# Three passes of rounded parts in the second layer's input projection, with two modulation chunks moved into the first layer's output projection

## The reference

```python
def first_block(x, c, ctx, c_ctx, w_ada, b_ada, g_norm, w_in, ...):
    for l in range(DEPTH):
        mod_lat = silu_c @ w_ada[l] + b_ada[l]
        mod_ctx = silu_cc @ w_ada[l] + b_ada[l]
        x, ctx = _layer(x, ctx, mod_lat, mod_ctx, tabs, g_norm[l], w_in[l], ...)
    return _rms_norm(x, g_final)
```

## Time and profile before

| | |
|---|---|
| runs | 1577.1 us median of 3 (1576.3 to 1580.47) |
| profiled execution, its own time | 1567.37 us |
| its span | 1565.6 us |
| granted TensorE clock, mean | 0.974 of full |
| busy share PE, DVE, ACT, POOL | 95%, 65%, 44%, 12% |
| second layer's input projection | 394.3 to 520.0 us |

### The profile page before, as it was taken

One profiled execution on the slowest core, in us unless ns is written; L12 is line 12 of the kernel. 1 busy time (PEld: TensorE's weight loads), 2 busy tenths in 40 slices (PEclk: granted clock), 3 DMA queues, 4 the chain that ended last, 5 costly groups with the idle time before them and its releaser, 6 DMA issues.

```text
span 1565.6 us, 19696 instructions
## 1 busy us (share of the span) xinstructions
PE 1481.6 (95%) x7621; PEld 1092.2 (70%) x7621; DVE 1010.9 (65%) x1587; ACT 695.9 (44%) x1125; POOL 192.0 (12%) x208
## 2 busy tenths in 40 slices
PE   5999997999999899999999999999999998899999
PEld 2777782554655455788778877878887876768886
DVE  2419747752475854677677768587786556477776
ACT  3311228322211631656146623466666657356654
POOL 1558721000000100200210010000000005000000
PEclk8999999999999989999999999899999999999999
DMA  9585611202484431766686654198884530098882
GB/s 339 193 259 199 223 62 55 82 1 98 145 293 160 165 121 55 234 215 219 189 238 233 224 172 105 55 324 297 311 302 139 188 108 1 1 307 305 292 305 108
DMA packets 186474, 286.55 MB, mean 183 GB/s; under 512 B 13739, under 2 KB 95115, under 8 KB 186380
## 3 DMA queue, kind: packets, MB, share of 16 engines
q1 hardware_dynamic: 172080, 273.56, 50.7%
q0 software_dynamic: 13200, 8.84, 3.0%
q10 hardware_dynamic: 1100, 2.89, 0.5%
HBM read 283.77 MB, written 1.49 MB: 182 GB/s over the span
## 4 chain that ended last, share of the span: by engine, by line
PE 80%; DVE 10%; ACT 5%; DMA 2%; SPq 1%; issue 1%; POOL 0%; DVEq 0%; ACTq 0%; POOLq 0%
PE ps L1309 40%; PE ps L2853 9%; PE ps L2744 3%; PE ps L2871 3%; PE ps L2873 2%; PE ps L2872 2%; DVE acc L2197 2%; DMA ring<-in_w_ada 2%; ACT ps L2045 2%; SPq L421 1%; PE ps L2777 1%; PE ps L2756 1%; PE ps L2765 1%; PE ps L2942 1%; PE ps L2982 1%
## 5 line engine op out<-in xcount | busy, mean ns | idle before, releaser
L1309 PE MATMUL ps<-WB,YP 128*128 128x512 f32 x1196 | 289.5, 396 | 2.7 <-DVE WB L2152 2.7
L1309 PEld LDWEIGHTS ps<-WB,YP 128*128 128x128 f32 x1196 | 228.0, 192 | 51.0 <-issue 2.2
L2152 DVE TENSOR_TENSOR WP<-ring,WP 128x2048 fp32r<-128x2048 f32 (+1 forms) x102 | 219.2, 2164 | 49.0 <-ACT WP L797 48.9
L1309 PE MATMUL ps<-WP,XP 128*128 128x512 f32 x960 | 233.1, 396 | 6.2 <-DVE WP L2152 6.2
L1309 PEld LDWEIGHTS ps<-WP,XP 128*128 128x128 f32 x960 | 178.8, 189 | 44.9 <-DVE XP L2152 4.9
L797 ACT ACTIVATE WP<-ring 128x2048 fp32r<-128x2048 f32 x94 | 179.5, 1914 | 38.2 <-PE ps L1309 38.2
L2152 DVE TENSOR_TENSOR WB<-ring,WB 128x512 fp32r<-128x512 f32 x192 | 128.0, 690 | 85.0 <-ACT WB L651 83.2
L2853 PE MATMUL ps<-ring,XT 128*128 128x512 f32 (+3 forms) x448 | 159.7, 511 | 2.6 <-ACT XT L1988 2.6
L651 ACT ACTIVATE WB<-ring 128x512 fp32r<-128x512 f32 x192 | 114.1, 628 | 53.9 <-PE ps L1309 53.9
L2853 PEld LDWEIGHTS ps<-ring,XT 128*128 128x128 f32 x448 | 81.7, 190 | 71.7 <-issue 63.6
L2197 DVE SCALAR_TENSOR_TENSOR acc<-ring,silu_c,acc 128x512 f32<-128x512 f32 x168 | 126.9, 756 | 4.4
(11 more groups left out here) (406 smaller groups left out, 2190.1 us busy)
## 6 DMA issues: line engine op xcount, KB each, us to landing
ring<-in_w_ada SPq DMA_DIRECT2D x72, 1024.0 KB, 7.4
ring<-in_a_w_in SPq DMA_DIRECT2D x36, 1024.0 KB, 5.0
ring<-in_w_gate SPq DMA_DIRECT2D x64, 512.0 KB, 4.2
ring<-in_w_up SPq DMA_DIRECT2D x64, 512.0 KB, 5.2
ring<-in_w_down SPq DMA_DIRECT2D x32, 1024.0 KB, 6.1
ring<-in_w_in SPq DMA_DIRECT2D x24, 1024.0 KB, 9.5
ring<-in_b_w_in SPq DMA_DIRECT2D x12, 1024.0 KB, 5.0
ring<-in_w_out SPq DMA_DIRECT2D x8, 1024.0 KB, 5.1
```

Source lines behind the costliest of these rows:

```text
L1309: ins = mm(dst, x(a), w(b), start=(start and n == 0), stop=(stop_ and n == 2))
L2152: return v.tensor_tensor(out_, a, b, op)
```

## The change

Chunks 2 to 6 of the second layer's projection (SPLIT = 2) are made in three passes of rounded parts, one weight block after the other for all tiles (`project_split_late`). ACT rounds the blocks (`high`) into 14 buffers (WH, the new WX, and XL, which lies on XT), DVE subtracts (`low`) into the ring slot itself; ACT also rounds the input into XH and DVE writes its low part (XL1) into unused columns of P. The blocks for chunk k + 1 are written into ACT's and DVE's queues ahead of chunk k's evictions and post-processing; those for chunk 2 behind the modulation of chunk 1. Modulations 3 and 4 move into the first layer's output projection, whose outputs now run through all tiles for the first 512 columns and then for the second; 5 to 9 stand behind chunks 0 to 4.

```diff
-               {0: (('ada2', 0, 3),), 1: (('ada2', 0, 4),), 2: (('ada2', 0, 5),), 3: (('ada2', 0, 6),), 4: (('ada2', 0, 7),), 5: (('ada2', 0, 8),), 6: (('ada2', 0, 9),)})
+               {n: (('ada2', 0, 5 + n),) for n in range(5)})
+MODS_OUT = (3, 4)
+SPLIT = 2
+HIGHS = 14
+def output_order(tiles):
+    return [(t, n) for n in range(2) for t in tiles] if len(tiles) == T else [(t, n) for t in tiles for n in range(2)]
...
     for n in range(2):
         chunk("wout", 0, n * 512, n * 512 + 512)
+    for c in MODS_OUT:
+        chunk("ada2", 0, c * 512, c * 512 + 512)
...
+                    if CHUNKS.index(it[2:4]) >= SPLIT:
+                        released.append(("w1_used", 7 * (CHUNKS.index(it[2:4]) - SPLIT) + 4))
...
+        W1H = [WH[:, n] for n in range(4)] + [WX[:, 0:512], WX[:, 512:1024]] + [XL[:, k] for k in range(KB)]
+        XL1 = [PH[:, at:at + 512] for at in (n + col for n in (0, D_IN) for col in (0, 512, BZ, CO))]
...
+                def high(r):
+                    it, w, hi, _ = win1_block(r)
+                    if r % 4 == 0:
+                        item_ready(act, it)
+                    if r == 6:
+                        act.wait_ge(*chunk_projected(SPLIT - 1))
+                        act.wait_ge(S("xt_lo"), 2 * KB)
+                    if r >= HIGHS:
+                        act.wait_ge(*win1_block_used(r - HIGHS))
+                    s_.activation(hi, w, ACT.Copy).then_inc(S("w1_hi"), 1)
+                for k in range(KB) if l == 1 else ():
+                    act.wait_ge(S("xt_act" if k % 2 == 0 else "xt_dve"), 4 + k // 2 + 1)
+                    s_.activation(XH[:, k], XT[:, k], ACT.Copy).then_inc(S("xt_hi"), 1)
                 for k, (lo, hi) in enumerate(CHUNKS):
+                    if l == 1 and SPLIT <= k < 6:
+                        for n in range(8):
+                            high(8 * (k + 1 - SPLIT) + n)
...
+                ops = (ada_ops("ada2", 0, ch) for ch in MODS_OUT)
+                for i, (t, n) in enumerate(output_order(tiles)):
+                    if len(tiles) == T:
+                        if i in (0, 5):
+                            chunk_ops = next(ops)
+                        for _ in range(0 if i in (4, 7) else 2 if i < 4 else 4):
+                            next(chunk_ops, None)
...
+                def low(r):
+                    _, w, hi, lo = win1_block(r)
+                    dve.wait_ge(S("w1_hi"), r + 1)
+                    tt(lo, w, hi.bitcast(F32), ALU.subtract).then_inc(S("w1_lo"), 1)
...
                 for k, (lo, hi) in enumerate(CHUNKS):
+                    if l == 1 and SPLIT <= k < 6:
+                        for n in range(8):
+                            low(8 * (k + 1 - SPLIT) + n)
                     for kind, layer, ch in MODS_BEHIND[l].get(k, ()) if l == 1 else ():
                         ada(kind, layer, ch)
+                    if l == 1 and k == 0:
+                        for n in range(KB):
+                            dve.wait_ge(S("xt_hi"), KB + n + 1)
+                            tt(XL1[n], XT[:, n], XH[:, n].bitcast(F32), ALU.subtract).then_inc(S("xt_lo"), 1)
+                    if l == 1 and k == SPLIT - 1:
+                        for n in range(6):
+                            low(n)
...
+            def project_split_late(n, behind):
+                lo_, hi_ = CHUNKS[n]
+                tiles = [(t, (lo_, hi_) if t >= 2 else CTX_LAST[n]) for t in range(T) if t >= 2 or CTX_LAST[n]]
+                us = [c.up("proj") - 1 for _ in tiles]
+                for k in range(KB):
+                    r = 8 * (n - SPLIT) + k
+                    _, _, hi, lo = win1_block(r)
+                    if n == SPLIT:
+                        pe.wait_ge(S("xt_lo"), KB + k + 1)
+                    pe.wait_ge(S("w1_lo"), r + 1)
+                    for (t, (a, e)), u in zip(tiles, us):
+                        if k == 0:
+                            pe.wait_ge(S("evict"), u - 3)
+                        b, cols, part = bank(u % 4, 0, e - a), slice(128 * t, 128 * t + 128), slice(a - lo_, e - lo_)
+                        mm(b, XH[:, k, cols], hi[:, part], start=(k == 0), stop=False)
+                        mm(b, XH[:, k, cols], lo[:, part], start=False, stop=False)
+                        ins = mm(b, XL1[k][:, cols], hi[:, part], start=False, stop=(k == KB - 1))
...
+                    if n == SIDE_CHUNK[1] and k in (1, 3, 5):
                         behind[k // 2]()
...
+                    pe.wait_ge(S("outp_used"), c.at("outp"))
                     norm_by_tile(range(T), before_last=5, before_chunks=3)
...
-                    if l == 1 and k > 0:
-                        ada(1)
-                    if l == 1 and k == 6:
+                    if l == 1 and k - 1 in MODS_BEHIND[1]:
                         ada(1)
```

More of the change, by code:

```diff
@@ L2094, in block1 @@
                             evict(P[:, t, rng[0]:rng[1]], lambda b, r=rng: b[:, 0:r[1] - r[0]])
+                        if l == 1 and k == SPLIT - 1 and t >= 2:
+                            for n in range(6) if t == 2 else range(6, 8):
+                                high(n)
                     if k < 6:
@@ L2494, in out_proj @@
                 dve.wait_ge(S("gate_rows_sb"), c.up("gate_rows_sb", len(set(side(t) for t in tiles))))
[L2495 to L2505, removed]
+                ops = (ada_ops("ada2", 0, ch) for ch in MODS_OUT)
[5 more added lines that the diff above has]
+                            next(chunk_ops, None)
+                        if i in (3, 6):
+                            a = c.up("ada") - 1
+                            pending.append(("ada2", 0, MODS_OUT[i // 4], a, bank(6 + a % 2, 0, 8)))
+                        if i in (5, 7):
+                            ada_cols()
+                    u = c.up("outp") - 1
+                    dve.wait_ge(S("outp"), u + 1)
+                    x = X[:, t, n * 512:n * 512 + 512]
+                    to("outp_used", tt(Ef[:, 0:512], bank((u + 2) % 4), GR[:, side(t), n * 512:n * 512 + 512], ALU.mult))
+                    ins = tt(x, x, Ef[:, 0:512], ALU.add)
+                    if n == 0:
+                        link(ins)
+                    else:
+                        to("x_tile", ins)
+                        (behind or (lambda t: invert_rstd([t])))(t)
             def twice_inverted(t):
@@ L2561, in block1 @@
                     dve.wait_ge(S("evict"), c.up("evict", units))
+                    if l == 1 and k == SPLIT - 1:
+                        low(6)
+                        low(7)
                     if before[1]:
@@ L2987, in out_proj @@
                 pe.wait_ge(S("evict"), c.at("proj"))
[L2988 to L2991, removed]
-                        if u - outp0[0] >= 4:
-                            pe.wait_ge(S("outp_used"), u - 3)
-                        b = bank((u + 2) % 4)
-                        if last_blocks and u == outp0[0]:
-                            project(b, t, its, 0, 512, 512, lhs=lhs, blocks=range(6))
-                            last_blocks()
-                            pe.wait_ge(S("evict"), c.at("proj"))
-                            ins = project(b, t, its, 0, 512, 512, lhs=lhs, blocks=range(6, 8))
-                        else:
-                            ins = project(b, t, its, 0, 512, 512, lhs=lhs)
-                        ins.then_inc(S("outp"), 1)
+                for i, (t, n) in enumerate(output_order(tiles)):
+                    its = [index[(kind, l, n * 512, n * 512 + 512, h)] for h in range(2)]
+                    u = c.up("outp") - 1
+                    if u - outp0[0] >= 4:
+                        pe.wait_ge(S("outp_used"), u - 3)
+                    b = bank((u + 2) % 4)
+                    if last_blocks and u == outp0[0]:
+                        project(b, t, its, 0, 512, 512, lhs=lhs, blocks=range(6))
+                        last_blocks()
+                        pe.wait_ge(S("evict"), c.at("proj"))
+                        ins = project(b, t, its, 0, 512, 512, lhs=lhs, blocks=range(6, 8))
+                    else:
+                        ins = project(b, t, its, 0, 512, 512, lhs=lhs)
+                    ins.then_inc(S("outp"), 1)
+                    if len(tiles) == T and i in (4, 6):
+                        ada(1)
                 outp0[0] = c.at("outp")
@@ L3111, in block1 @@
                         project_split(k, behind)
-                    for t in range(T) if l == 1 else ():
+                    elif k >= SPLIT:
+                        project_split_late(k, behind)
+                    for t in range(T) if l == 1 and k < SPLIT else ():
                         r = (lo, hi) if (l == 0 or t >= 2) else CTX_LAST[k]
```

23 lines of the change are left out of this document (18 added, 5 removed).

## The result

The changed kernel took 1585.4 us (median of 4 runs, 1582.9 to 1586.6) against 1576.7 for the kernel before: ratio 1.0048, 95% interval 1.0028 to 1.0068. It is slower, by 8.7 us where 12.3 were forecast, and measured again beside other runs by 9.6 us (first experiment). The profiled execution took 1582.94 us, span 1581.1.

A forecast was written before the change was run, and what follows sets the result against it. The prediction took DVE's chain, not PE, to bound chunks 3 and 4: 17.6 us late inside chunk 5, less 7.0 PE saving, plus 1.8 clock, sum +12.3. On the 1577.1 us median that gave 1589 us, range 1580 to 1598.

The forecast's parts named there:

- The rival that PE decides: PE, not DVE, sets the time in the projection's chunks: faster, -16.3 us, 1561 us; chance 0.10.
- the 16 us that the passes were to save: Chunks 2 to 6: three rounded passes replace exact products, PE work falls from 82.8 to 66.5 us, by 16.3.
- Start of chunk 0: Output projection's two added column sums (+1.6 us) and 0.3 of a new wait: chunk 0 starts at 396.2, not 394.3.
- Chunks 0 and 1: Both stay exact, 31.6 us, to 427.8; PE then waits 1.0 us and starts chunk 2 at 429.6.
- DVE up to the norm: Subtractions for chunks 2 and 3 and a modulation precede the query/key norm on DVE: it starts 7.7 us late.
- mis-sized term: DVE's idle time waiting for chunk 3's weights, ahead of the norm: 4 us.
- PE's wait: Before chunk 4, whose subtractions stand behind the 17.7 us norm on DVE: PE idle 14.9 us.
- To the side steps: Norm's end to PE's release inside chunk 5: 26.4 us plus 9.9 of subtractions; PE waits some 10 us.
- The rest: PE from inside chunk 5 to the transposes behind chunk 6: 27.0 us instead of 34.0, plus 1.8 for low clock.
- The upper bound of +19: Whole change: full 0.69 us subtractions (+2.9), weights 2 us later, second clock loss on the chain (+1.8).
- the lower one: Whole change: +6.5 us, without the clock term and with weights early enough that DVE does not idle.
- The cover of the moved modulations: First layer's output projection: two modulations fit DVE's idle time, costing nothing there; at most 3.1 us if it failed.

The follow-up runs named there:

- first experiment: The changed kernel measured again, unedited: 1585.3 us, ratio 1.0079; beside it, the modulations' move alone with exact products in all chunks: 1572.7 us.
- Experiment 6: Changed kernel with side steps in chunk 6 and modulation 7 before chunk 3's subtractions, plus chunk 4's subtractions put inside the norm: 1572.2 us, ratio 0.9991.
- experiment 2: Changed kernel with modulation 7 ahead of chunk 3's eight subtractions in DVE's queue: 1584.2 us, ratio 1.0065.
- experiment 3: Changed kernel with nine unused exact products put into PE's wait inside chunk 5: 1581.8 us, ratio 1.0047.

## Why the prediction was right, and where it was off

The direction, the cause and the places hold: DVE ends last in this stretch, PE's saving turns into PE's waits, and the DVE work put ahead of the norm counts in full. The rival that PE decides falls: PE's busy time in the whole profile fell from the value in the earlier trace rows to 1471.9 us, its share from 95% to 93%, and the time rose. From chunk 2 to the transposes PE was busy 90.86 us before and 77.67 after; of the 16 us that the passes were to save 1.6 more left with two column sums, and some 4.5 came back as products at low clock (0.92 in the mean from 470 to 488.8 us, 0.90 from 504.8 to 534.7).

The prediction read the rule of the Trainium skill's page "Perfetto Trace Analysis", section "Identifying the Most-Contended Engine", as pointing to PE. By PE's busy share it does, but for PE the page asks for MFU and the share of the weight loads (PEld). By PEld PE leads only over the whole span (70% against DVE's 65%). In chunk 3 PEld has 6.54 of 14 us and in chunk 4 13.33 of 22, against DVE's 12.13 and 19.03. So read stage by stage, and by the weight loads, the rule names DVE, and this case agrees with it.

Experiment 6 is the sharpest test: DVE's order changed and its total didn't, a PE wait shrank by 6 us, and the stretch stayed.

Step by step, by the stretch (counted from the first output product, which came 1.9 us earlier in the trace after; those 1.9 us are added to the times of the trace here):

1. *Start of chunk 0*: 396.2 forecast, 394.26 + 1.9 = 396.2. Right, by the size too.
2. *Chunks 0 and 1*: forecast 31.6 us as before. They took 33.3 (394.26 to 427.57). This step failed by 1.7 us, and its cause is the clock, which I had not charged here: the granted clock was 0.50 from 398 to 400 us and 0.66 from 400 to 402, which makes 1.7 us of lost time (last section). PE's wait of 1.0 at chunk 2 was 1.09.
3. *DVE up to the norm*: the norm was to start 7.7 us late and started 11.1 late (451.04 + 1.9 against 441.81): 1.9 from step 2, and some 1.5 because the weights came later (two loads of this kind took 11.4 us to land in the median). I took 4 us for DVE's idle time from a median of three loads of that kind; it was 5.96. This is the **mis-sized term** that lies in my own working, and experiment 2, which filled the gap, won it back.
4. *PE's wait*: 14.9 forecast, 15.93 measured. The norm took 17.7 us, as before.
5. *To the side steps*: 26.4 + 9.9 = 36.3 forecast, 36.2 measured (468.72 to 504.88). The wait inside chunk 5: some 10, measured 9.75 and 8.2.
6. and 7. *The rest*: 27.0 + 1.8 = 28.8 forecast, 29.9 measured. With PE kept busy it was 27.3, so the work itself was sized right, and the clock costs 2.6 us or more instead of 1.8.

The sum by the trace is +16.6 us in the stretch where 12.3 were forecast: +1.9 from step 2, +1.5 from step 3, +1.0 from step 7, less 0.1. The upper bound of +19 held; the lower one took the weights in time, and they were late. The cover of the moved modulations held: the prediction had DVE idle 5.45 us before each output, which is so for five of the eight (5.2 to 5.5; 3.6 to 3.7 before the others), and after the change it still idles 0.5 us or more before each.

On the medians it is 8.7 and 9.6, less than the forecast, while the profiled executions differ by 15.6 (1567.37 to 1582.94). That the time came within 4 us of the forecast is in part luck: the stretch lost 4.3 us more than forecast, and the medians moved 6 to 7 us less than the traces. Here the prediction's way from one execution to the median failed: it added the trace's difference to a median 9.7 us above its trace, as if that gap were the same in both kernels. It is not. The two traced executions of the kernel before had a mean granted clock of 0.974 and 0.975; over its 100 timed executions with a recorded clock, those at 0.9655 to 0.9685 took 1579.9 us in the mean and those above 0.9755 took 1570.2. The changed kernel's lie at 0.959 to 0.970, the traced ones too (0.969, 0.967), and its traces stand 1 to 2.5 us from its median. So part of its low clock is spent in waits, where PE has nothing to lose, as the stretch of 453 to 470 us shows with PEclk 0.59 and PE busy 1.07 us. That the kernel before in its turn loses PE time in its usual executions at places that its two traces don't show is my reading and not shown: no trace of a slower execution of it was taken. Part of that loss is gone with the moved modulations already, without the passes: the median less the stretch is 1382.9 to 1385.0 us for the kernel before, 1380.4 for the moved modulations alone and 1374.9 to 1377.1 for the changed kernel. The other versions' traces show that an execution can lose such time outside the stretch: in that of experiment 3, 7.8 us above its median, the first output product comes at 335.77 us in place of 326.4 to 331.0.

## What to carry to other kernels

Where two engines are both nearly full over a stretch, follow the chain of waits before spending on one of them. Work taken from the other was worth nothing here, and the work that the saving needs (here the low parts, 0.6 us each on DVE) lands on the one that decides. Then the order on that engine is worth more than the saving: two moves without any new work took back 13 us of the changed kernel. And compare like stretches between traces as well as medians, since a profiled execution may stand 8 us from its kernel's median.

## What the runs showed that I had not expected

**POOL and DVE hold each other up.** With both on operations with two inputs from SBUF, DVE's modulation took 10.84 us instead of 5.48 and a 128x128 product 1.24 instead of 0.29, about the length of one POOL subtraction (1.26); POOL's went to 1.66. DVE's sums with one input kept their time. "POOL is idle here" is no cover for moving such work to it while DVE is on the chain.

**The clock fell at chunk 0, where PE had hardly waited.** The first 8 us of chunk 0, first with the modulations moved only, then in the kernel before (second trace):

```profile
397.00:401.00 4.00, 3.98 (x35) 3.95 (x35) 3.82 (x6) 0.37 (x2) 0.00 (x0) 1.00 1.07 390
401.00:405.00 4.00, 4.00 (x12) 3.04 (x11) 1.77 (x3) 0.00 (x0) 0.00 (x0) 0.59 0.64 237
```

```profile
393.00:397.00 4.00, 3.99 (x33) 3.43 (x31) 3.86 (x7) 0.61 (x2) 0.00 (x0) 1.00 0.02 4
397.00:401.00 4.00, 4.00 (x20) 3.37 (x20) 2.30 (x4) 0.18 (x1) 0.00 (x0) 1.00 0.00 0
```

In every trace with the modulations moved chunks 0 and 1 took 33.3 us (35.0 once), with the clock near 0.6 some 5 us into chunk 0, and in both traces of the kernel before 31.6. Of what differs ahead of it I saw two things: one wait of 0.9 us at the end of the output projection, and the loads of the weights, which now run beside chunk 0's start (390 GB/s against 4). I can't tell whether the clock follows either of the two; no run separated them.
